# First feed-forward products with the high and low activations in one 512-column matmul

## The chip, the cores and the metric

One core of one Trainium2 chip runs the whole program. The metric is device time in microseconds (us), the median over several runs; lower is better. The profile beside it is one execution.

## The reference, cut to what matters

Two transformer-like blocks run one after the other on 256 rows of 2048 numbers, all in 32-bit floats. Both end with the same feed-forward, and only these two are touched:

```python
h2 = rms_norm(x, norm2_w) * (1.0 + scale2) + shift2      # 256 x 2048
f  = jnp.square(jax.nn.relu(h2 @ w_ff1)) @ w_ff2         # 2048 -> 8192 -> 2048
x  = x + gate2 * f
```

Shift, scale and gate come from `silu(c) @ w_ada`, one row times a 2048 x 12288 matrix for each block (the modulation). Before the feed-forwards stand the input projections, pooling and stick-breaking attention in the first block, dilated attention and a gated recurrence in the second, and their output projections.

## The kernel before, in words

**Precision.** TensorE multiplies numbers of the format fp32r, which keeps fewer bits than a 32-bit float. So each operand is split into a high part (rounded to fp32r) and a low part (the rest), and a product is taken as high x high + high x low + low x high: three matmuls that accumulate in PSUM. For the weights ScalarE (ACT in the profile) makes the high part `WH` by a copy (line 1000), and VectorE (DVE) makes the low part `WL` by a subtraction (line 1367). Lines 598, 1000, 1367 and 1375 are helpers, so they stand for nearly all matmuls, activations, tensor-tensor operations and scalar-tensor-tensor operations.

**The stream of weights.** All weights come in chunks of 256 x 512 numbers (512 KB), 848 of them, numbered j. SyncE issues their DMAs into a ring of raw buffers (`RAW`, `RAWX`, `RAWY`; six slots, four from chunk 434 to 591). The split halves have three slots each (a fourth in part of the second block). On every engine the program is one loop over j. ACT and DVE split chunk j+2 (`feed`, `look`) in their round j; ACT waits for the slot, that is, for PE to have finished chunk j-1. The modulation's weights travel in the same raw ring, as chunks that DVE multiplies by a column of `silu(c)` and adds up (`ACC<-RAW,CS,ACC`, line 1375); `weight_plan` spreads them over the weights: over the first 240 chunks of the first feed-forward in five groups with pauses, over the first 160 of the second in one.

**Blocks.** `block_table` lists the output blocks. A block of the second product (`ff2`, `fg2`) is 4 chunks and has rows of x as its output partitions: activations are stationary, weights move, 512 columns a matmul (`chunk`). A block of the first product (`ff1`, `fg1`) is 8 chunks and comes out transposed (`chunk_t`): weights are stationary (128 x 128), and the 256 rows of activations move, so each (k, i) step of a chunk is three matmuls of 256 columns (WH with high, WH with low, WL with high). Its output of 512 x 256 fills two PSUM banks, two i to a bank. `Blocks` gives each block a pair of banks, 0-1 and 2-3 in turn; banks 4 to 7 serve the side work (transposes, attention, recurrence). `prev` says which block had the pair before, and `bank_free` makes PE wait until that one was read.

**Order in a feed-forward.** Two blocks of the first product come first; then eight rounds: two blocks of the first product for the next round (none in the last round), then four blocks of the second product, which use what the first product made a round earlier. So 16 chunks of the one kind and 16 of the other take turns, and the last 32 chunks are all of the second kind.

**What happens to a finished block.** `ended(j)` hands the two halves (t = 0, 1) of a block to `evac` in the two rounds after its last chunk. For the first product ACT does Relu from PSUM into `rl`, Square into the high part `AH`, Square into `fs` (full precision), and DVE subtracts into the low part `AL`. For the second product DVE adds the PSUM bank to `acc` (in the first round of four ACT copies it there), and in the last rounds multiplies by the gate and adds into x.

**The norm before a feed-forward.** x is normalised, transposed on PE into banks 4 to 7 tile by tile (`turn_rows`), scaled and shifted by DVE into `hn` (`norm_tile`), copied as high part by ACT and subtracted as low part by DVE (`norm_low`); the first block's chunk c waits for the tile it uses.

Of the kernel before, what the change touches and what calls it, by code (L numbers as in the profile page):

```python
# [110 lines left out]
def f32(ap):  # L111
    return ap.bitcast(F32)
# [167 lines left out]
def reader(name, n):  # L280

    if name == "in1":
        return "dve" if n > 0 else "act"
    if name in ("oa", "ff1", "fg1"):
        return "act"
    if name in ("ff2", "fg2"):
        return "act" if n < 4 else "dve"
    if name == "in2":
        return "dve" if IN2_ORDER[n] // 2 in (3, 6) else "act"
    return "dve"  # L290


class Blocks:


    def __init__(self):
# [4 lines left out]
        self.sum_of, self.head = [], []  # L301
        counts, owner, pair, parts = {"act": 0, "dve": 0}, {}, 0, {}
        for q, (name, n, at, ticks) in enumerate(self.all):
            if (name, n) == ("in1", 0):
                b, pair = 0, 1
                self.first = q
            else:
                b = 2 * (pair % 2) + (2 if at < 64 else 0)
                pair += 1
            eng = reader(name, n)  # L310
            self.sum_of.append(parts.get(n) if name in ("part", "in1") else None)
            if name == "part":
                if n not in parts:
                    eng = "act"
# [6 lines left out]
            self.prev.append(owner.get(b))  # L321
            owner[b] = q
            self.by_end[at + ticks - 1] = q
            self.at[name, n] = q
# [21 lines left out]
def program(nc, I, C, out):  # L346
# [3 lines left out]
    with ExitStack() as ctx:  # L350
# [43 lines left out]
        def ff_memory(tag, stack):  # L394
            h = sb("BH" + tag, [128, KT, S], F32R, stack)
            l = sb("BL" + tag, [128, KT, S], F32R, stack)
            xn = sb("xn" + tag, [128, 2, D], F32, stack)
            hn = sb("hn" + tag, [128, 4, 256], F32, stack)
            acc = sb("acc" + tag, [128, 2, D], F32, stack)
            rl = sb("rl" + tag, [128, 2, 512], F32, stack)  # L400
            fs = sb("fs" + tag, [128, 2, 512], F32, stack)
            tmp = sb("tmp" + tag, [128, 2, 512], F32, stack)
            return {"h": h, "l": l, "xn": xn, "hn": hn, "acc": acc, "rl": rl, "fs": fs, "tmp": tmp}

# [98 lines left out]
        def vc(name, t=0):  # L503
# [24 lines left out]
            "cols", "sqrt", "rows0", "rows1", "turned", "mod", "hi", "lo")]  # L528
        s_fs, s_fl, s_fp = sem("f_square"), sem("f_lo"), sem("f_gated")
        s_ct, s_lb, s_lbe, s_gs, s_f, s_ln = (sem("ct_rounded"), sem("lb_step"), sem("lb_exp"), sem("gate_sigmoid"),  # L530
# [64 lines left out]
        def _(e):  # L595
# [7 lines left out]
            def bank_free(q, t):  # L603

                before = bl.prev[q]
                if before is not None:
                    eng, count = evac_of[before][t]
                    e.wait_ge(s_ev[eng], count)
# [16 lines left out]

            def chunk_t(j, q, c, hi, lo):
# [329 lines left out]
            for j in range(AUP, NW):  # L956
# [7 lines left out]
                if name in ("ff1", "fg1"):  # L964
                    mem, base = (M1, FF) if name == "ff1" else (M2, FG)
                    if n == 0:
                        e.wait_ge(s_nl, 8 * norms[base][0] + c + 1)
                    chunk_t(j, q, c, mem["h"], mem["l"])
                elif name in ("ff2", "fg2"):
# [27 lines left out]
        def _(e):  # L997
# [46 lines left out]
            def evac(q, t):  # L1044
# [3 lines left out]
                if name in ("in1", "part"):  # L1048
# [12 lines left out]
                    elif name == "in1" and n >= 12:  # L1061
                        g_b = SB[:, t, (n - 12) * 512:(n - 11) * 512]
                        e.wait_ge(s_ev["dve"], evac_of[q][t][1])
                        af(g_b, g_b, ACT.Sigmoid).then_inc(s_sgb, 1)
                elif name in ("ff1", "fg1"):
                    mem, base = (M1, 0) if name == "ff1" else (M2, 32)
                    r = n // 2
                    i = base + 2 * n + t
                    k = 8 * (r % 2) + 4 * (n % 2) + 2 * t
                    e.wait_ge(s_wdone, done_at)  # L1070
                    if n > 0:
                        e.wait_ge(s_fl, i - 1)
                    af(mem["rl"][:, t, :], ps, ACT.Relu).then_inc(s_ev["act"], 1)
                    e.wait_ge(s_ev["act"], evac_of[q][t][1])
                    af(AH[:, k:k + 2, :].rearrange("p a b -> p (a b)"), mem["rl"][:, t, :], ACT.Square)
                    af(mem["fs"][:, t, :], mem["rl"][:, t, :], ACT.Square).then_inc(s_fs, 1)
                elif name in ("ff2", "fg2") and n < 4:
# [20 lines left out]
                elif name == "oa":  # L1098
# [3 lines left out]
                    af(HG[:, 1 + n // 2, t, (n % 2) * 512:(n % 2) * 512 + 512], ps, ACT.Copy).then_inc(s_ev["act"], 1)  # L1102

            def squares(name, n, t):

# [17 lines left out]
            def norm_tile(at, i):  # L1123
                inst, _, _, hn, hi, _ = norms[at]
                e.wait_ge(s_nv, 16 * inst + 2 * i + 2)
                src = hn[:, 2 * i % 4:2 * i % 4 + 2, :].rearrange("p a s -> p (a s)")
                af(hi[:, 2 * i:2 * i + 2, :].rearrange("p a s -> p (a s)"), src, ACT.Copy).then_inc(s_nh, 1)

# [220 lines left out]
            for j in range(NW + 3):  # L1349
# [14 lines left out]
        def _(e):  # L1364
# [117 lines left out]
            def evac(q, t):  # L1482
# [35 lines left out]
                elif name in ("ff1", "fg1"):  # L1518
                    mem, base = (M1, 0) if name == "ff1" else (M2, 32)
                    k = 8 * (n // 2 % 2) + 4 * (n % 2) + 2 * t  # L1520
                    two = slice(k, k + 2)
                    e.wait_ge(s_fs, base + 2 * n + t + 1)
                    tt(AL[:, two, :].rearrange("p a b -> p (a b)"), mem["fs"][:, t, :],
                       f32(AH[:, two, :]).rearrange("p a b -> p (a b)"), ALU.subtract).then_inc(s_fl, 1)
                elif name in ("ff2", "fg2") and n >= 4:
# [49 lines left out]
                elif name == "ob":  # L1575
# [3 lines left out]
                    add_x("ob", n, t, ps, o, ev)  # L1579

            def gated_first(n, t):

# [19 lines left out]
            def norm_low(at, i):  # L1602
                inst, _, _, hn, hi, lo = norms[at]
                e.wait_ge(s_nh, 8 * inst + i + 1)
                two = slice(2 * i, 2 * i + 2)
                src = hn[:, 2 * i % 4:2 * i % 4 + 2, :].rearrange("p a s -> p (a s)")
                tt(lo[:, two, :].rearrange("p a s -> p (a s)"), src, f32(hi[:, two, :]).rearrange("p a s -> p (a s)"),
                   ALU.subtract).then_inc(s_nl, 1)

# [301 lines left out]
            for j in range(NW + 3):  # L1911
# [9 lines left out]
                else:  # L1921
# [143 lines left out]
```

## Time and profile before

| | us |
|---|---|
| median of 3 runs (2688.21 to 2689.26) | 2688.37 |
| profiled execution | 2683.85 |
| its span, first to last instruction | 2682.1 |
| PE busy | 2547.7 (95%) |
| DVE busy | 2000.3 (75%) |
| ACT busy | 1273.0 (47%) |

Engines: PE is TensorE's matmuls, PEld its weight loads, DVE is VectorE, ACT ScalarE, POOL GpSimd. Matmuls are pipelined and the printed lengths of neighbours overlap; the distance between two starts is the pace. An arrow reads output <- inputs, with the names of the program's tiles (`BH` and `BL` are the high and low activations here, `PS` is PSUM). The names of an instruction's tiles tell the stage: `PS<-BH,WH` is the first product, `PS<-WH,AH` the second product or another one with moving weights. In the chain of waits, "issue" is time for which the profile shows no reason.

### The profile page before, as it was taken

To read this page: it belongs to the slowest core of one execution; us is meant where nothing else is said; L and a number is where in the kernel's file an instruction comes from. 1 tells how busy PE (TensorE), PEld (TensorE's weight loads), DVE (VectorE), ACT (ScalarE), POOL (GpSimd) and SP (SyncE) were. 2 spreads that over 40 slices of the span, in tenths; PEclk is the share of its full clock that TensorE was granted. 3 is DMA by queue.
4 is the path that set the end of the run, shared out by engine and by line. 5 is a ranking of instruction groups with operands and counts; after the bars stand their busy time and mean duration, and the time that the engine had idled before them with its cause. 6 is when DMAs were issued, how large, how long until landed. Compare 5 with 4: busy or idle time off the path is not lost.

```text
span 2682.1 us, 36228 instructions
## 1 busy us (share of the span) xinstructions
PE 2547.7 (95%) x14307; PEld 2220.3 (83%) x14307; DVE 2000.3 (75%) x2232; ACT 1273.0 (47%) x1590; POOL 278.1 (10%) x323
## 2 busy tenths in 40 slices
PE   5999999998999999999989999888899999999998
PEld 4777777777999989998867788767799998999897
DVE  6788858998877888788888677876765566565556
ACT  4544395344454444444445544345445444444443
POOL 0000120202030201001030002451000000020000
PEclk9999999999999999999999999999999999999999
DMA  8998849997888989897965645666567777766664
GB/s 312 316 335 323 275 154 342 322 329 251 298 291 308 319 297 332 267 354 259 329 196 175 180 134 149 196 218 205 192 186 227 226 223 228 226 216 191 190 183 147
DMA packets 298218, 663.88 MB, mean 248 GB/s; under 512 B 20753, under 2 KB 20849, under 8 KB 297025
## 3 DMA queue, kind: packets, MB, share of 16 engines
q1 hardware_dynamic: 294976, 650.21, 72.9%
q0 software_dynamic: 2784, 10.05, 1.1%
q8 instruction: 113, 1.85, 0.3%
q10 hardware_dynamic: 288, 1.31, 0.1%
q14 instruction: 57, 0.46, 0.0%
HBM read 659.39 MB, written 2.10 MB: 247 GB/s over the span
## 4 chain that ended last, share of the span: by engine, by line
PE 75%; DVE 11%; issue 4%; DMA 4%; ACT 4%; POOL 1%; SPq 0%; DVEq 0%; ACTq 0%
PE PS L598 75%; DVE WL L1367 3%; DVE ACC L1375 3%; ACT WH L1000 2%; DMA RAW<-in_w_in 2%; DVE UQ L1367 1%; DMA RAWX<-in_w_ada 1%; DVE hn L1372 1%; PE PS L601 1%; DMA RAW<-in_w_o 0%; ACT L1000 0%; DMA RAWX<-in_w_a_up 0%; DVE acc L1367 0%; ACT UQ L1000 0%; DVE AL L1367 0%
## 5 line engine op out<-in xcount | busy, mean ns | idle before, releaser
L1367 DVE TENSOR_TENSOR WL<-RAW,WH 128x1024 fp32r<-128x1024 f32 x567 | 706.6, 1247 | 404.2 <-ACT WH L1000 403.7
L1000 ACT ACTIVATE WH<-RAW 128x1024 fp32r<-128x1024 f32 x567 | 600.8, 1060 | 831.4 <-PE PS L598 646.4
L598 PE MATMUL PS<-WH,AH 128*128 128x512 f32 x2052 | 815.5, 397 | 25.8 <-DVE WL L1367 12.4
L598 PE MATMUL PS<-WL,AH 128*128 128x512 f32 x2052 | 802.9, 391 | 0.0
L598 PE MATMUL PS<-WH,AL 128*128 128x512 f32 x2052 | 802.7, 391 | 0.0
L598 PE MATMUL PS<-BH,WH 128*128 128x256 f32 x2048 | 583.0, 285 | 5.1 <-DVE BL L1367 5.1
L598 PE MATMUL PS<-BH,WL 128*128 128x256 f32 x2048 | 581.4, 284 | 0.0
L598 PE MATMUL PS<-BL,WH 128*128 128x256 f32 x2048 | 581.4, 284 | 0.0
L598 PEld LDWEIGHTS PS<-WH,AH 128*128 128x128 f32 x2052 | 387.8, 189 | 116.8 <-DVE WL L1367 25.9
L598 PEld LDWEIGHTS PS<-WH,AL 128*128 128x128 f32 x2052 | 387.2, 189 | 82.3
L598 PEld LDWEIGHTS PS<-WL,AH 128*128 128x128 f32 x2052 | 387.7, 189 | 77.7 <-issue 1.0
L598 PEld LDWEIGHTS PS<-BH,WH 128*128 128x128 f32 x2048 | 394.9, 193 | 8.7 <-DVE BL L1367 8.2
L598 PEld LDWEIGHTS PS<-BL,WH 128*128 128x128 f32 x2048 | 394.9, 193 | 0.5
L598 PEld LDWEIGHTS PS<-BH,WL 128*128 128x128 f32 x2048 | 394.8, 193 | 0.0
L1375 DVE SCALAR_TENSOR_TENSOR ACC<-RAW,CS,ACC 128x1024 f32<-128x1024 f32 x265 | 338.6, 1279 | 2.5 <-DMA RAW<-in_w_ada 1.7
L1965 POOL PARTITION_ALL_REDUCE ACC<-ACC x72 | 156.0, 2250 | 1339.5 <-DVE ACC L1375 1339.5
L1000 ACT ACTIVATE WH<-RAWX 128x1024 fp32r<-128x1024 f32 x150 | 158.9, 1060 | 201.9 <-PE PS L598 131.3
L1367 DVE TENSOR_TENSOR WL<-RAWX,WH 128x1024 fp32r<-128x1024 f32 x150 | 187.7, 1252 | 63.0 <-ACT WH L1000 62.5
L1367 DVE TENSOR_TENSOR WL<-RAWY,WH 128x1024 fp32r<-128x1024 f32 x96 | 117.6, 1225 | 81.8 <-ACT WH L1000 81.8
L1000 ACT ACTIVATE WH<-RAWY 128x1024 fp32r<-128x1024 f32 x96 | 101.8, 1061 | 139.7 <-PE PS L598 136.4
L1375 DVE SCALAR_TENSOR_TENSOR ACC<-RAWX,CS,ACC 128x1024 f32<-128x1024 f32 x95 | 121.4, 1278 | 5.6 <-DMA RAWX<-in_w_ada 5.5
L598 PE MATMUL PS<-WX,AH 128*128 128x512 f32 x248 | 77.5, 394 | 2.1 <-DVE AL L1367 2.1
(241 smaller groups left out, 2033.3 us busy)
## 6 DMA issues: line engine op xcount, KB each, us to landing
RAW<-in_w_ff SPq DMA_DIRECT2D x335, 512.0 KB, 4.6
RAW<-in_w_ada SPq DMA_DIRECT2D x284, 512.0 KB, 5.1
RAW<-in_w_in SPq DMA_DIRECT2D x192, 512.0 KB, 4.5
RAWX<-in_w_ada SPq DMA_DIRECT2D x100, 512.0 KB, 5.5
RAWY<-in_w_ff SPq DMA_DIRECT2D x96, 512.0 KB, 4.5
RAWX<-in_w_ff SPq DMA_DIRECT2D x81, 512.0 KB, 5.0
RAWX<-in_w_in SPq DMA_DIRECT2D x48, 512.0 KB, 5.3
RAW<-in_w_out SPq DMA_DIRECT2D x32, 512.0 KB, 4.3
```

Source lines behind the costliest of these rows:

```text
L598: return e.matmul(o, l, r, start=start, stop=stop, skip_group_check=True)
L601: return e.transpose(o, i, ident)
L1000: return e.activation(o, i, f, **kw)
L1367: return e.tensor_tensor(o, a, b, op)
L1372: return e.tensor_scalar(o, a, s1, s2, op0, op1)
L1375: return e.scalar_tensor_tensor(out=o, in0=a, scalar=s, in1=b, op0=op0, op1=op1)
L1965: e.partition_all_reduce(part, part, 128, bass.bass_isa.ReduceOp.add).then_inc(s_red, 1)
```

## The change

The high and the low activations of the feed-forward lie side by side in one tile `HL`, so that for each k the 256 high and the 256 low columns are one run of 512. `chunk_t` sends both through WH in one matmul of 512 columns, whose output is a whole bank, and the high ones through WL in a second matmul of 256 columns, which adds to the first half of that bank. The low activations' share thus stands in the second half, apart. A block takes one bank for each i, four in all: 0 to 3 or 4 to 7 in turn; the blocks of the second product rotate over all eight banks. After a block ACT copies the second halves of two banks to `rl`, DVE adds the first halves to them in place, ACT takes Relu in place and both Squares a round later (`ff_square`), and DVE subtracts into `AL` two rounds later (`ff_low`). The second block of each feed-forward waits until the norm has read banks 4 to 7. The norm's copies and subtractions write into `HL` in two runs of 256.

```diff
@@ reader @@
-    if name in ("oa", "ff1", "fg1"):
+    if name == "oa":
         return "act"
@@ Blocks.__init__ @@
+            elif name in ("ff1", "fg1"):
+                b = 4 * (n % 2)
+            elif name in ("ff2", "fg2"):
+                b = 2 * (n % 4)
...
+            if name in ("ff1", "fg1"):
+                self.prev.append([owner[b // 2 + t][1] for t in range(2)])
+                for t in range(2):
+                    owner[b // 2 + t] = [self.ev[q][t]] * 2
+            else:
+                self.prev.append(owner[b // 2])
+                owner[b // 2] = self.ev[q]
@@ ff_memory @@
-            h = sb("BH" + tag, [128, KT, S], F32R, stack)
-            l = sb("BL" + tag, [128, KT, S], F32R, stack)
+            hl = sb("HL" + tag, [128, KT, 2, S], F32R, stack)
@@ tensor: chunk_t @@
-                        o = PS[:, b + i // 2, (i % 2) * 256:(i % 2) * 256 + 256]
-                        mm(o, h, hi[:, k, :], k == 0 and i % 2 == 0, False)
-                        mm(o, h, lo[:, k, :], False, False)
-                        m = mm(o, l, hi[:, k, :], False, k == KT - 1)
+                        mm(PS[:, b + i, :], h, both[:, k, :, :].rearrange("p a s -> p (a s)"), k == 0, False)
+                        m = mm(PS[:, b + i, 0:256], l, both[:, k, 0, :], False, k == KT - 1)
@@ tensor: main loop @@
+                    elif n == 1 and c == 0:
+                        e.wait_ge(s_nv, 16 * norms[base][0] + 16)
@@ scalar: evac @@
-                    if n > 0:
-                        e.wait_ge(s_fl, i - 1)
-                    af(mem["rl"][:, t, :], ps, ACT.Relu).then_inc(s_ev["act"], 1)
-                    e.wait_ge(s_ev["act"], evac_of[q][t][1])
-                    af(AH[:, k:k + 2, :].rearrange("p a b -> p (a b)"), mem["rl"][:, t, :], ACT.Square)
-                    af(mem["fs"][:, t, :], mem["rl"][:, t, :], ACT.Square).then_inc(s_fs, 1)
+                    two = PS[:, bl.bank[q] + 2 * t:bl.bank[q] + 2 * t + 2, 256:512]
+                    if n > 0:
+                        e.wait_ge(s_fs, base + 2 * n + t - 1)
+                    af(mem["rl"][:, t, :].rearrange("p (a s) -> p a s", s=256), two, ACT.Copy).then_inc(s_fc, 1)
+            def ff_square(q, t):
...
+                e.wait_ge(s_ev["dve"], evac_of[q][t][1])
+                af(mem["rl"][:, t, :], mem["rl"][:, t, :], ACT.Relu).then_inc(s_fr, 1)
+                e.wait_ge(s_fr, i + 1)
+                af(AH[:, k:k + 2, :].rearrange("p a b -> p (a b)"), mem["rl"][:, t, :], ACT.Square)
+                if n > 0:
+                    e.wait_ge(s_fl, i - 1)
+                af(mem["fs"][:, t, :], mem["rl"][:, t, :], ACT.Square).then_inc(s_fs, 1)
@@ scalar: loop, after feed(j + look(j)) and before evac @@
+                for q, t in bl.ended(j - 1):
+                    if bl.all[q][0] in ("ff1", "fg1"):
+                        ff_square(q, t)
@@ vector: evac @@
-                    e.wait_ge(s_fs, base + 2 * n + t + 1)
-                    tt(AL[:, two, :].rearrange("p a b -> p (a b)"), mem["fs"][:, t, :],
-                       f32(AH[:, two, :]).rearrange("p a b -> p (a b)"), ALU.subtract).then_inc(s_fl, 1)
+                    two = PS[:, bl.bank[q] + 2 * t:bl.bank[q] + 2 * t + 2, 0:256]
+                    low = mem["rl"][:, t, :].rearrange("p (a s) -> p a s", s=256)
+                    e.wait_ge(s_fc, base + 2 * n + t + 1)
+                    tt(low, two, low, ALU.add).then_inc(s_ev["dve"], 1)
@@ vector: loop, after feed and before evac; ff_low holds the subtraction removed above @@
+                    for q, t in bl.ended(j - 2):
+                        if bl.all[q][0] in ("ff1", "fg1"):
+                            ff_low(q, t)
```

## Rows read from the trace of the kernel before

**Rows 1.** The page's busy time (us, share of the span, instructions) of each engine.
```profile
PE 2547.7 (95%) x14307; PEld 2220.3 (83%) x14307; DVE 2000.3 (75%) x2232; ACT 1273.0 (47%) x1590; POOL 278.1 (10%) x323
```

**Rows 2.** The chain that ended last: start, us, what; its two longest pieces.
```profile
693.07 612.87 PE PS L598 x4080
...
1972.95 699.94 PE PS L598 x4464
```

**Rows 3.** The same chain from 640 to 720: one period of the head.
```profile
679.90 0.99 DVE hn L1372 x2
...
681.49 1.08 DVE ACC L1375
...
683.74 0.99 DVE hn L1372 x2
```

**Rows 4.** Stretches: length, then busy us (count) by engine, PE clock, DMA share, GB/s.
```profile
669.00:672.00 3.00, 3.00 (x14) 3.00 (x15) 2.99 (x5) 0.63 (x1) 0.00 (x0) 0.50 0.00 0
...
768.04:811.59 43.55, 43.55 (x195) 36.06 (x193) 27.56 (x25) 23.15 (x28) 20.79 (x8) 1.00 0.75 250
811.59:857.66 46.07, 46.07 (x385) 46.07 (x384) 35.38 (x32) 21.23 (x24) 0.00 (x0) 1.00 0.92 315
...
1126.52:1170.07 43.55, 43.55 (x195) 36.05 (x193) 40.27 (x39) 20.15 (x22) 0.00 (x0) 1.00 0.99 355
...
1259.69:1305.76 46.07, 46.07 (x385) 46.07 (x384) 37.51 (x34) 20.27 (x22) 0.00 (x0) 1.00 0.97 346
1305.76:1353.90 48.14, 44.62 (x195) 35.69 (x193) 46.75 (x49) 20.25 (x22) 5.42 (x3) 1.00 0.80 272
...
1972.95:2672.90 699.95, 699.92 (x4464) 639.68 (x4464) 413.02 (x391) 319.19 (x353) 20.08 (x14) 1.00 0.67 208
```

**Rows 5.** PE in order of time: start us, length us, operation; where widths change.
```profile
669.34 0.41 PE L598 MATMUL PS<-BL,WH 128*128 128x256 f32 x1
669.55 0.41 PE L598 MATMUL PS<-BH,WL 128*128 128x256 f32 x1
...
767.92 0.28 PE L598 MATMUL PS<-BH,WL 128*128 128x256 f32 x1
768.04 0.40 PE L598 MATMUL PS<-WH,AH 128*128 128x512 f32 x1
...
811.36 0.39 PE L598 MATMUL PS<-WH,AL 128*128 128x512 f32 x1
811.59 0.28 PE L598 MATMUL PS<-BH,WH 128*128 128x256 f32 x1
...
1601.95 1.05 PE L598 MATMUL PS<-QP,KP 128*128 128x128 f32 x8
```

**Rows 6.** DVE in order of time in a busy stretch, and PE's matmul after it.
```profile
1151.63 0.68 DVE L1367 TENSOR_TENSOR acc<-PS,acc 128x512 f32<-128x512 f32 x1
1152.23 1.27 DVE L1375 SCALAR_TENSOR_TENSOR ACC<-RAWX,CS,ACC 128x1024 f32<-128x1024 f32 x1
1153.42 1.22 DVE L1367 TENSOR_TENSOR WL<-RAW,WH 128x1024 fp32r<-128x1024 f32 x1
1154.56 0.68 DVE L1367 TENSOR_TENSOR acc<-PS,acc 128x512 f32<-128x512 f32 x1
...
1156.38 1.23 DVE L1367 TENSOR_TENSOR WL<-RAW,WH 128x1024 fp32r<-128x1024 f32 x1
...
1159.19 0.39 PE L598 MATMUL PS<-WH,AH 128*128 128x512 f32 x1
```

**Rows 7.** ACT in order of time, the end of a first-product block.
```profile
1130.79 0.58 ACT L1000 ACTIVATE rl<-PS 128x512 f32<-128x512 f32 x1
1131.40 0.63 ACT L1000 ACTIVATE AH<-rl 128x512 fp32r<-128x512 f32 x1
1131.93 0.61 ACT L1000 ACTIVATE fs<-rl 128x512 f32<-128x512 f32 x1
1132.45 1.04 ACT L1000 ACTIVATE WH<-RAWX 128x1024 fp32r<-128x1024 f32 x1
```

More of the change, by code:

```diff
@@ L301, in __init__ @@
         self.sum_of, self.head = [], []
-        counts, owner, pair, parts = {"act": 0, "dve": 0}, {}, 0, {}
+        counts, owner, pair, parts = {"act": 0, "dve": 0}, [[None, None] for _ in range(4)], 0, {}
         for q, (name, n, at, ticks) in enumerate(self.all):
@@ L320, in __init__ @@
             counts[eng] += 2
-            self.prev.append(owner.get(b))
-            owner[b] = q
+            if name in ("ff1", "fg1"):
[5 more added lines that the diff above has]
+                owner[b // 2] = self.ev[q]
             self.by_end[at + ticks - 1] = q
@@ L402, in ff_memory @@
             tmp = sb("tmp" + tag, [128, 2, 512], F32, stack)
-            return {"h": h, "l": l, "xn": xn, "hn": hn, "acc": acc, "rl": rl, "fs": fs, "tmp": tmp}
+            return {"hl": hl, "h": hl[:, :, 0, :], "l": hl[:, :, 1, :], "xn": xn, "hn": hn, "acc": acc, "rl": rl, "fs": fs, "tmp": tmp}
         phase = ExitStack()
@@ L528, in program @@
             "cols", "sqrt", "rows0", "rows1", "turned", "mod", "hi", "lo")]
-        s_fs, s_fl, s_fp = sem("f_square"), sem("f_lo"), sem("f_gated")
+        s_fc, s_fr, s_fs, s_fl, s_fp = sem("f_low_part"), sem("f_relu"), sem("f_square"), sem("f_lo"), sem("f_gated")
         s_ct, s_lb, s_lbe, s_gs, s_f, s_ln = (sem("ct_rounded"), sem("lb_step"), sem("lb_exp"), sem("gate_sigmoid"),
@@ L603, in bank_free @@
             def bank_free(q, t):
-                before = bl.prev[q]
+                before = bl.prev[q][t]
                 if before is not None:
-                    eng, count = evac_of[before][t]
+                    eng, count = before
                     e.wait_ge(s_ev[eng], count)
@@ L624, in chunk, with chunk_t @@
                 m.then_inc(s_wdone, 1)
-            def chunk_t(j, q, c, hi, lo):
+            def chunk_t(j, q, c, both):
                 e.wait_ge(s_lo, j + 1)
@@ L967, in _ @@
                         e.wait_ge(s_nl, 8 * norms[base][0] + c + 1)
-                    chunk_t(j, q, c, mem["h"], mem["l"])
+                    elif n == 1 and c == 0:
+                        e.wait_ge(s_nv, 16 * norms[base][0] + 16)
+                    chunk_t(j, q, c, mem["hl"])
                 elif name in ("ff2", "fg2"):
@@ L1102, in evac @@
                     af(HG[:, 1 + n // 2, t, (n % 2) * 512:(n % 2) * 512 + 512], ps, ACT.Copy).then_inc(s_ev["act"], 1)
+            def ff_square(q, t):
+                name, n = bl.all[q][:2]
+                mem, base = (M1, 0) if name == "ff1" else (M2, 32)
+                i = base + 2 * n + t
+                k = 8 * (n // 2 % 2) + 4 * (n % 2) + 2 * t
+                e.wait_ge(s_ev["dve"], evac_of[q][t][1])
[5 more added lines that the diff above has]
+                af(mem["fs"][:, t, :], mem["rl"][:, t, :], ACT.Square).then_inc(s_fs, 1)
             def squares(name, n, t):
@@ L1125, in norm_tile @@
                 e.wait_ge(s_nv, 16 * inst + 2 * i + 2)
-                src = hn[:, 2 * i % 4:2 * i % 4 + 2, :].rearrange("p a s -> p (a s)")
-                af(hi[:, 2 * i:2 * i + 2, :].rearrange("p a s -> p (a s)"), src, ACT.Copy).then_inc(s_nh, 1)
+                af(hi[:, 2 * i:2 * i + 2, :], hn[:, 2 * i % 4:2 * i % 4 + 2, :], ACT.Copy).then_inc(s_nh, 1)
             def norm_begin(at):
@@ L1579, in evac, with ff_low @@
                     add_x("ob", n, t, ps, o, ev)
+            def ff_low(q, t):
+                name, n = bl.all[q][:2]
+                mem, base = (M1, 0) if name == "ff1" else (M2, 32)
+                k = 8 * (n // 2 % 2) + 4 * (n % 2) + 2 * t
+                two = slice(k, k + 2)
+                e.wait_ge(s_fs, base + 2 * n + t + 1)
+                tt(AL[:, two, :].rearrange("p a b -> p (a b)"), mem["fs"][:, t, :],
+                   f32(AH[:, two, :]).rearrange("p a b -> p (a b)"), ALU.subtract).then_inc(s_fl, 1)
             def gated_first(n, t):
@@ L1605, in norm_low @@
                 two = slice(2 * i, 2 * i + 2)
-                src = hn[:, 2 * i % 4:2 * i % 4 + 2, :].rearrange("p a s -> p (a s)")
-                tt(lo[:, two, :].rearrange("p a s -> p (a s)"), src, f32(hi[:, two, :]).rearrange("p a s -> p (a s)"),
-                   ALU.subtract).then_inc(s_nl, 1)
+                tt(lo[:, two, :], hn[:, 2 * i % 4:2 * i % 4 + 2, :], f32(hi[:, two, :]), ALU.subtract).then_inc(s_nl, 1)
             def norm_begin(at):
```

5 lines of the change are left out of this document (removed).

## The prediction

> **What bounds the kernel now.** I read the busy table first: PE is busy 95% of the span, DVE 75%, ACT 47% [rows 1]. A share that high for PE is only a hint, so the chain of waits comes next. Its two longest pieces are PE alone: 612.87 us from 693.07, and 699.94 us from 1972.95, half of the span together [rows 2]. These are the two feed-forwards. In them nothing but the number and the spacing of the matmuls sets the time. Two stretches at their edges are different. At the head of each feed-forward, before 693 and before 1973, the chain runs through DVE: a normalised tile is scaled, its low part made, one modulation product added, in 3.8 us per chunk [rows 3]. (A chunk is one 256 x 512 piece of weights, a block is 8 chunks of the first product or 4 of the second.) At the tail of the first feed-forward, 1305.76 to 1353.90, DVE is busy 46.75 of 48.14 us and PE waits for it [rows 4].
>
> **The spacing of matmuls.** The lengths printed for matmuls overlap, so I take start-to-start spacings. Sixteen chunks of the first product are 384 matmuls of 256 columns in 46.07 us, 120.0 ns each; sixteen of the second are 192 of 512 columns in 43.55 us, 226.8 ns each [rows 4]. At the granted clock of 1.00 (2.4 GHz) the columns alone would take 106.7 and 213.3 ns. Both widths pay the same 13.3 to 13.5 ns on top, and both load their weights anew each time. So this is a surcharge per matmul, not per column. Where widths change, a 256 is followed after 0.12 us by a 512, and a 512 after 0.23 us by a 256 [rows 5], as in the uniform streams. Eight matmuls of 128 columns with own weights take 1.05 us [rows 5]: under 0.13 each, and some 0.11 when the overhang of the last is taken off, although their columns would take 0.053. That is the nearest thing to a floor from weight loading; it is under 0.12, so the loads still hide behind the 256-column stream, which the change keeps as the shortest one.
>
> **What the change takes from PE.** Before, each (k, i) step is three matmuls of 256 columns, 360.0 ns. After, it is one of 512 and one of 256, 226.8 + 120.0 = 346.8 ns: 13.2 ns less. A chunk has 8 such steps, 0.105 us of 2.88. Each feed-forward has 128 chunks of the first product. The first six run in the DVE-bound head, and the first of these at a granted clock of 0.50 [rows 4], where starts are 0.21 us apart, 256 columns at 1.2 GHz and no surcharge to save [rows 5]; I count nothing for them. That leaves 2 x 122 = 244 chunks, 1952 steps, 25.7 us. The bounds: with the boundary rows as printed, 0.23 + 0.12 = 0.35 us, a step saves 0.010 us, 19.5 us in all. More than 13.2 ns is excluded, because every width in the trace pays the surcharge. A gain below nothing is excluded for PE by itself, since no spacing gets longer than in the streams shown.
>
> The Trainium skill, "TensorE: Matmul & The Clock Gate", section "Back-to-back issue gap", gives a warm gap of N/2.4 + 2.5 ns. By that a step would save 2.5 ns and the whole 4.9 us. The trace does not agree: it has 13.3 ns over the stream in both widths [rows 4].
>
> **What it adds to ACT and DVE.** A block's end was, for each of two halves: ACT Relu from PSUM, Square into AH, Square into fs, then DVE's subtraction into AL. Now ACT first copies the low-part half-banks, DVE adds the other halves, ACT does Relu and both Squares one chunk later, and DVE's subtraction comes two chunks later. So each half adds one PSUM read on ACT (0.61 us from one start to the next, as the Relu has) and one PSUM addition on DVE (0.60 us, as acc<-PS,acc has) [rows 6, 7]. Per feed-forward that is 16 blocks x 2 x 0.60 = 19 us of DVE. In the second feed-forward DVE is busy 413 of 700 us [rows 4], and the weights' low parts are ready well ahead; cost nothing. In the first one there are modulation products besides, and the question is whether the low part WL of a chunk is still ready when PE wants it. The tightest place I found: WL ends at 1157.61 and PE begins that chunk at 1159.19, a lead of 1.6 us [rows 6].
>
> By hand, from the spacings of rows 6 and 7 (WL 1.14, product 1.19, addition or subtraction 0.60, weight copy 0.97 to 1.06, Relu 0.61, Squares 0.53 and 0.52), with a chunk every 2.72 us and a product in every one: let chunk A begin at 0. ACT copies weights until 1.3 and the low parts until 1.9; DVE adds until 3.2. In B, ACT has weights until 4.0, Relu and Squares until 5.6, the second copy until 6.2; DVE, ready before, waits 0.7 us for it and adds until 6.9. In C, ACT begins the weights at 6.2 instead of 5.7; DVE has the product until 8.0 and WL at 9.2, wanted at 10.9: lead 1.7. Then 1.5 in D, 1.3 in E, 1.0 in F, and 0.8 at the lowest, with the subtractions and the second product's additions in between. Products come in fewer than all chunks, so the lead recovers. Taken alone this gives no stall. What can turn it into one is late weights: in this very stretch the DMA engines are busy 0.99 at 355 GB/s. Products and first-product chunks together draw 346 GB/s at 2.88 us a chunk [rows 4]; at 2.775 that becomes 359, at what the queue was ever seen to hold (355 / 0.99 = 359). I allow 1.2 us of new PE waits there. The bounds are 0 (the rings of six raw and three split buffers take it up) and 8 us (0.5 us at each of 16 blocks).
>
> At the tail DVE is the chain, so what is added there is paid. The last first-product block ends at 1305.8, and its two additions fall into it: 2 x 0.60, with 0.1 for the later handover: 1.3 us, between 0 and 3.
>
> The banks: blocks of the first product now hold four banks, 0 to 3 or 4 to 7, and those of the second rotate over all eight. The owner before ended at least 8 chunks (22 us) earlier in each case, where it could be 4 before; in the norm stage banks 4 to 7 belong to the transposes until the second block, which waits for all 16 tiles. The last tile is done before the head ends, two chunks before that block begins. Nothing for either.
>
> **The sum.** 2683.85 (the profiled execution) - 25.7 + 1.3 + 1.2 = 2660.65 us. The median of the runs is 2688.37, 4.52 above the profiled execution, and I add that: 2665.2 us.
>
> **The rivals.**
> - *Half the gain is taken by weight delivery in the first feed-forward.* For it: the 355 GB/s above, and PE already gets along with a lead of 1.6 us. Against it: a group of products lasts about 37 chunks and then pauses, and the excess of demand over supply is under 1%. If it holds, the first feed-forward keeps its pace: 2688.4 - 12.9 + 1.3 = 2676.8.
> - *The surcharge is owed for each 256 columns, or is far smaller in a mixed stream.* Then the step is as long as before and only the tail moves: 2688.4 + 1.3 = 2689.7; with the page's 2.5 ns it would be 2684.8. Against it: 226.8 ns for 512 columns, where two surcharges would make 240.
> - *Slower: the new round trip ACT, DVE, ACT, DVE blocks ACT's weight copies.* ACT works in order, its Relu waits for DVE's addition, which stands behind a low part and a product, and the weight copy of the next chunk is queued behind. For it: DVE is busy 92 to 97% in the densest stretches [rows 4]. Against it: the leads above, and the second feed-forward has no products after its first 160 chunks. It decides from 0.8 us of PE waiting at every one of the 32 blocks (25.7 / 32). With 1.2 us at each, 2688.4 - 25.7 + 1.3 + 38.4 = 2702.4.
>
> **How the numbers follow.** The forecast has 0.84, weight delivery 0.08, the surcharge 0.03, slower 0.05. With everything at its best the forecast's case gives 2688.4 - 25.7 = 2662.7, with everything at its worst 2688.4 - 19.5 + 8 + 3 = 2679.9; its own range is 2661 to 2672, since the 4.5 us between profile and median may shift by a microsecond or two and the worst ends hardly meet. The range for 8 in 10 takes in a little of the second case: 2660.5 to 2673. A change of 0.2%, 5.4 us, is about what can be told from none here. Faster by more has the first two cases, 0.92; within it the third, 0.03; slower 0.05.
>
> **What would show it.** In the changed profile: sixteen chunks of the first product in 44.4 us instead of 46.07; a pair spacing of 0.23 and 0.12; PE busy without a gap from about 693, ending the long piece some 12.8 us sooner, and the second one shortened by the same. ACT's copies and DVE's additions 64 times each, near 0.58 and 0.68 us. The tail from the last first-product block to the norm longer than now by about 1.3 us. I am wrong on the size if sixteen chunks take more than 45 us, and on the mechanism if PE shows waits for WL after each first-product block.

## The result

The changed kernel takes 2669.45 us in the median of 4 runs (2666.06 to 2675.75), against 2688.29 us for the kernel before in the same comparison. The ratio is 0.9936, with a 95% interval of 0.9918 to 0.9954: 12 to 22 us less, where 23.2 were forecast (2665.2 us, range 2660.5 to 2673). The direction and the range held. The size of the main term did not: by the forecast's own sign (sixteen chunks over 45 us) it was wrong on the size.

The profile after: first the busy time of each engine (answers to [rows 1]), then the two longest pieces of the chain ([rows 2]).

```profile
PE 2536.4 (95%) x12259; PEld 2111.6 (79%) x12259; DVE 2035.6 (76%) x2296; ACT 1300.1 (49%) x1654; POOL 287.3 (11%) x323
```

```profile
696.22 611.98 PE PS L607 x3128
...
1972.57 692.22 PE PS L607 x3488
```

The 2048 matmuls taken away are there (14307 to 12259), and so are 35 us more of DVE. The second piece, which ends with the last chunk in both kernels, is 7.7 us shorter. The first can't be compared by its length, since it ends at another chunk. By chunks (198 to 415 in both) it went from 612.69 to 606.30 us. First the row of before, then those of after: the same chunks, then sixteen second-product chunks, sixteen first-product ones, two stretches of the second feed-forward, and the first half of the tail ([rows 4]).

```profile
693.07:1305.76 612.69, 612.69 (x4080) 567.75 (x4081) 496.85 (x462) 283.95 (x317) 71.75 (x32) 1.00 0.88 307
```

```profile
696.22:1302.52 606.30, 606.30 (x3105) 515.42 (x3106) 512.02 (x492) 296.61 (x347) 76.32 (x32) 1.00 0.88 309
...
769.81:813.34 43.53, 43.53 (x195) 36.05 (x193) 30.92 (x27) 23.97 (x30) 20.19 (x8) 1.00 0.74 250
813.34:858.55 45.21, 45.21 (x258) 39.22 (x256) 36.46 (x34) 22.14 (x26) 0.00 (x0) 1.00 0.92 315
2000.41:2044.79 44.38, 44.38 (x259) 38.82 (x258) 28.09 (x27) 25.17 (x32) 0.00 (x0) 1.00 0.73 226
2088.33:2133.54 45.21, 45.21 (x258) 39.23 (x256) 25.86 (x24) 22.03 (x26) 0.00 (x0) 1.00 0.71 224
1302.52:1352.93 50.41, 45.00 (x194) 35.57 (x193) 48.14 (x51) 21.07 (x24) 5.41 (x3) 1.00 0.78 273
```

PE is busy without a gap in all stretches but the tail. Yet sixteen chunks of the first product take 45.21 us, not 44.4: only 0.86 us less than before. One stretch, from 2000.41, takes 44.38, exactly as forecast. The same instructions thus ran at two paces, at the same granted clock of 1.00. PE in order of time shows them (start, length, operation). First the slow one; three steps of a 512 and a 256 take 1.06 us (719.63 to 720.69), 353 ns each, and the 512s keep the next matmul away for 0.24, 0.24 and 0.23 us:

```profile
719.63 0.40 PE L607 MATMUL PS<-HL,WH 128*128 128x512 f32 x1
719.87 0.28 PE L607 MATMUL PS<-HL,WL 128*128 128x256 f32 x1
719.99 0.40 PE L607 MATMUL PS<-HL,WH 128*128 128x512 f32 x1
720.23 0.28 PE L607 MATMUL PS<-HL,WL 128*128 128x256 f32 x1
720.34 0.40 PE L607 MATMUL PS<-HL,WH 128*128 128x512 f32 x1
720.57 0.28 PE L607 MATMUL PS<-HL,WL 128*128 128x256 f32 x1
720.69 0.40 PE L607 MATMUL PS<-HL,WH 128*128 128x512 f32 x1
```

In the fast one two steps take 0.69 us (2009.77 to 2010.46), 346 ns each:

```profile
2009.77 0.40 PE L607 MATMUL PS<-HL,WH 128*128 128x512 f32 x1
2010.00 0.28 PE L607 MATMUL PS<-HL,WL 128*128 128x256 f32 x1
2010.12 0.39 PE L607 MATMUL PS<-HL,WH 128*128 128x512 f32 x1
2010.35 0.27 PE L607 MATMUL PS<-HL,WL 128*128 128x256 f32 x1
2010.46 0.40 PE L607 MATMUL PS<-HL,WH 128*128 128x512 f32 x1
```

In nanoseconds the spacings repeat as 241, 120, 236, 113, 233, 117 in the slow rhythm (1060 for three steps) and as 231, 112, 233, 117 in the fast one (693 for two). Over sixteen chunks that is 353.2 and 346.7 ns a step. In this profile 26 of the 244 chunks ran in the fast one.

### The profile page after: what moved, and what is told of

It is laid out like the page before. It is cut to its first block, busy times and chain, and to the rows that moved or that the text cites. A ratio compares the mean times of both kernels' runs of the same rounds, so it can differ in the third digit from the quotient of the medians.

```text
span 2674.0 us, 32260 instructions
## 1 busy us (share of the span) xinstructions
PE 2536.4 (95%) x12259; PEld 2111.6 (79%) x12259; DVE 2035.6 (76%) x2296; ACT 1300.1 (49%) x1654; POOL 287.3 (11%) x323
## 4 chain that ended last, share of the span: by engine, by line
PE 77%; DVE 9%; ACT 4%; issue 4%; DMA 4%; POOL 1%; SPq 0%; DVEq 0%; ACTq 0%
PE PS L607 76%; DVE WL L1388 2%; DVE ACC L1396 2%; ACT WH L1010 2%; DMA RAW<-in_w_in 2%; DVE UQ L1388 1%; DMA RAWX<-in_w_a_up 1%; PE PS L610 1%; DMA RAWX<-in_w_ada 1%; DVE hn L1393 1%; POOL NT L1974 1%; ACT L1010 0%; POOL NT L1979 0%; DVE acc L1388 0%; ACT UQ L1010 0%
## 5 line engine op out<-in xcount | busy, mean ns | idle before, releaser
L607 PE MATMUL PS<-HL,WH 128*128 128x512 f32 x2048 | 728.7, 400 | 5.6 <-DVE HL L1388 5.6
L607 PE MATMUL PS<-HL,WL 128*128 128x256 f32 x2048 | 576.2, 281 | 0.0
L607 PEld LDWEIGHTS PS<-HL,WH 128*128 128x128 f32 x2048 | 386.9, 189 | 104.1 <-DVE HL L1388 9.0
L607 PEld LDWEIGHTS PS<-HL,WL 128*128 128x128 f32 x2048 | 388.8, 190 | 0.5
L1995 POOL PARTITION_ALL_REDUCE ACC<-ACC x72 | 162.2, 2336 | 1325.9 <-DVE ACC L1396 1325.9
L1974 POOL TENSOR_SCALAR NT<-SM 128x4 f32<-128x4 f32 (+2 forms) x14 | 16.0, 1141 | 470.3 <-DVE SM L1399 411.7
L1388 DVE TENSOR_TENSOR acc<-PS,acc 128x512 f32<-128x512 f32 x96 | 65.6, 683 | 0.0
```

The source lines that it names most:

```text
L607: return e.matmul(o, l, r, start=start, stop=stop, skip_group_check=True)
L1388: return e.tensor_tensor(o, a, b, op)
L1974: e.tensor_scalar(o, a, s1, s2, ALU.mult, ALU.add).then_inc(s_rs, 1)
L1995: e.partition_all_reduce(part, part, 128, bass.bass_isa.ReduceOp.add).then_inc(s_red, 1)
```

## The experiments

Their timings belong to three comparisons with the kernel before, whose medians lay at 2686.4 us (the first four experiments), 2687.7 (the next four) and 2687.0 (the last four). Single runs have no interval, so only their profiles are used. In what follows "sixteen chunks" is the length of a first-product stretch in the profile.

**The same kernel again.** No edit.

> The changed kernel once more. In its first profile a pair of matmuls (512 and 256 columns) took 346.3 ns in the first 26 chunks of the second feed-forward and 353.2 ns in the other 218, where 346.8 was forecast. Theory A (the alternation of widths has two steady rhythms, and which one a stretch gets is chance): the profile again has stretches at 2.77 and at 2.83 us a chunk, but elsewhere; the times scatter over some 10 us as before (2666 to 2676), since all fast against all slow is 244 x 0.055 = 13 us. Theory B (the rhythm is fixed by the place in the program): the same 26 chunks are fast again, the rest slow, and the times scatter by 2 us only.

Measured: 2669.62 us (4 runs, 2668.95 to 2674.14), ratio 0.9942 (0.9927 to 0.9957). The first 26 chunks of the first feed-forward, slow before, were fast now (44.38 us, first row), the first 26 of the second fast again, and every later stretch slow in both profiles:

```profile
721.70:766.08 44.38, 44.38 (x259) 38.81 (x258) 40.49 (x39) 25.17 (x32) 0.00 (x0) 1.00 0.97 345
809.68:854.88 45.20, 45.20 (x257) 39.20 (x256) 36.44 (x34) 22.15 (x26) 0.00 (x0) 1.00 0.91 314
```

So neither theory holds whole: the stretches entered from the head of a feed-forward have either rhythm, and the twelve entered from the second product's 512s always had the slow one. What the rhythm can explain between two runs is 2 x 26 chunks, 2.7 us at most. The other scatter is older than the change: the kernel before ranged from 2680.22 to 2691.34 us over 13 runs in this comparison, and the first 192 chunks, which the change doesn't touch, took 624.7 to 630.7 us in all the profiles, counted from the first matmul with weights.

**The block end alone.** The merged matmul is split into two again.

```diff
-                        mm(PS[:, b + i, :], h, both[:, k, :, :]..., k == 0, False)
+                        mm(PS[:, b + i, 0:256], h, both[:, k, 0, :], k == 0, False)
+                        mm(PS[:, b + i, 256:512], h, both[:, k, 1, :], False, False)
                         m = mm(PS[:, b + i, 0:256], l, both[:, k, 0, :], False, k == KT - 1)
```

> The changed kernel with its merged matmul undone: WH with the high columns and WH with the low columns are again two matmuls of 256 columns, into the two halves of the bank. Banks, copies, additions and their delays stay as changed. This is the cost of the new block end by itself. Theory A and B alike: chunks at 2.880 us in all of both feed-forwards, no scatter, and against the kernel before only the tail of the first feed-forward grows: 1.3 us forecast, 1.9 seen in the first profile; 2689 to 2691 us. Rival C (the new block end also slows matmuls beside it, through the shared banks): chunks longer than 2.880 us near the block ends, over 2692 us.

Measured: 2689.48 us (10 runs) against 2686.38 (13 runs), ratio 1.0011 (1.0001 to 1.0021), 0.3 to 5.6 us slower. All stretches are those of the kernel before, and the tail is longer:

```profile
817.10:863.17 46.07, 46.07 (x385) 46.06 (x384) 36.20 (x33) 22.14 (x26) 0.00 (x0) 1.00 0.91 309
1311.27:1361.33 50.06, 44.96 (x194) 35.58 (x193) 48.03 (x51) 21.08 (x24) 5.40 (x3) 1.00 0.79 271
```

The new block end slows no matmul beside it, so rival C falls. Nor do the new banks: with them a stream of 256s still takes 46.07 us. The whole gain comes from the merged matmul. The first half of the tail is 1.7 to 1.9 us longer than in the two profiles of before; the rest of this profile's 9 us over the first of them lies mostly in the first 192 chunks (5.0) and the heads (1.3), which scatter.

**Four 512s, then four 256s.** The second matmul moves into a loop of its own over i.

> As the changed kernel, but for each k the four matmuls of 512 columns come first and the four of 256 after them, so widths change twice in eight matmuls instead of eight times. Theory A (the alternation has the slow rhythm): chunks at 8 x (226.8 + 120.0) = 2.774 us in nearly all stretches, so 218 x 0.055 = 12 us less than the changed kernel's profile, 2662 to 2666 us, and little scatter. Rival D (the surcharge grows for another reason, as for a moving operand read twice in a row or for the state of the chip): still 2.83 us in most stretches, 2668 to 2676 us.

Measured: 2666.7 us (4 runs), ratio 0.9931 (0.9915 to 0.9948). Sixteen chunks take 44.88 us in every stretch but the first of each feed-forward (44.91), half-way between. Both theories had it wrong: grouping helps, but a run of four 512s behind 256s is spaced 233, 236, 228, 233 or 235, 234, 236, 224 ns, so it does not settle at 226.7.

**The 256 first in each pair.**

> As the changed kernel, but in each pair the 256 columns with WL come first and the 512 with WH second. Theory A: the same alternation, so both rhythms are possible again, 2.77 or 2.83 us a chunk, 2664 to 2677 us with scatter. Rival E (what costs is that a matmul of 256 follows one of 512 into the same bank): the 256 now precedes the 512 of its bank and follows one of another bank, and all chunks take 2.774 us, 2662 to 2666 us.

Measured: 2674.41 us (4 runs, 2667.96 to 2675.55), ratio 0.9951 (0.9937 to 0.9966). Sixteen chunks take 45.22 us in all fourteen stretches. Rival E falls: the slow pace stays where the 256 no longer follows the 512 of its own bank.

The row of the fours, then that of the 256 first:

```profile
808.69:853.57 44.88, 44.88 (x257) 39.24 (x256) 35.91 (x33) 22.15 (x26) 0.00 (x0) 1.00 0.90 314
```

```profile
815.25:860.47 45.22, 45.22 (x257) 39.21 (x256) 36.12 (x33) 22.15 (x26) 0.00 (x0) 1.00 0.92 313
```

**The kernel before again.** No edit.

> The kernel before once more, for a second profile of it. The changed kernel and its first variants showed the first chunk of both feed-forwards at 5.2 to 5.7 us against 4.97 and 4.87 in the one profile of before, and 193 to 194 us for the first 64 chunks of the program against 191.7. Theory A (these parts have nothing to do with the change and scatter): they differ again, the first chunk over 5.2 us. Theory B (the change costs half a microsecond at each head): 4.9 us again. Both: every first-product chunk at 2.880 us.

Measured: 2686.78 us (one run). Theory A: the first chunk of the second feed-forward took 5.82 us up to the next one's start this time, as long as the longest with any variant of the change (5.83), and that of the first 4.83. How long PE stays at a granted clock of 0.50 after the gap there is scatter:

```profile
812.55:858.62 46.07, 46.07 (x386) 46.07 (x385) 35.62 (x32) 21.24 (x24) 0.00 (x0) 1.00 0.90 315
1306.72:1355.06 48.34, 44.69 (x194) 35.65 (x193) 46.83 (x49) 20.26 (x22) 5.41 (x3) 1.00 0.79 269
1951.28:1957.10 5.82, 5.82 (x29) 5.82 (x29) 2.73 (x4) 0.88 (x3) 0.00 (x0) 0.52 0.31 90
```

In two profiles of variants (the mirrored pairs, and the last one of eights) one of the two first chunks had a granted clock of 1.00 throughout and took 3.3 us. The one of the mirrored pairs:

```profile
670.50:673.76 3.26, 3.26 (x21) 2.88 (x21) 3.21 (x5) 0.74 (x3) 0.00 (x0) 1.00 0.02 5
```

**Mirrored pairs.** For odd i the 256 comes first, then the 512.

> The changed kernel with every second pair turned round: 512, 256, 256, 512, 512, 256, 256, 512. Widths change four times in eight matmuls instead of eight. Where four 512s stood together (and two changes in eight) a chunk took 2.805 us, at eight changes 2.83 or 2.77. If each change of width costs the same, this lies between, 2.81 to 2.82 us a chunk, 45.1 us for sixteen. If it is a beat of the sequence as a whole, it can be anything from 2.774 up, and the spacings repeat in a pattern of their own.

Measured: 2665.13 us (one run). Sixteen chunks take 44.58 us, less than with fours. Four changes of width cost less than two did, so it is no fixed price per change but depends on the whole sequence; the spacings repeat every four steps, a pattern of their own, as the second expectation had it.

```profile
809.28:853.86 44.58, 44.58 (x257) 38.94 (x256) 36.43 (x34) 22.12 (x26) 0.00 (x0) 1.00 0.92 316
```

**Eight 512s, then eight 256s.** One loop over both k and all i for the 512s, one for the 256s.

> All eight 512s of a chunk first, then its eight 256s: two changes of width in sixteen matmuls. If the extra time sits in the first few matmuls after a change (in the variant with fours a 512 after the 256s is 233 to 236 ns from the next, in the second product it settles at 226.7 after about five), a chunk takes 2.79 us and the median is 2664 to 2667 us. If it stays for as long as 256s are in the mix, 2.80 to 2.83 us as with fours or alone, 2667 to 2671 us.

Measured: 2663.08 us (4 runs), ratio 0.9914 (0.9898 to 0.9929). Sixteen chunks take 44.66 us, 2.79 us each, as the first expectation said: after 256s the 512s stand 232, 236, 228, 233 and 231 ns apart and then 226 to 227, with the 256s at 120 again after two.

```profile
809.39:854.05 44.66, 44.66 (x257) 39.35 (x256) 36.44 (x34) 22.12 (x26) 0.00 (x0) 1.00 0.91 318
```

**Entry from 256s.** The first chunk of the first of two blocks is three matmuls of 256 columns.

> The changed kernel, but the first chunk of each pair of first-product blocks is three matmuls of 256 columns again, so the alternation is entered from a stream of 256s, not from the 512s of the second product. Every stretch entered from 512s had the slow rhythm (2.83 us a chunk) in three profiles, those entered from the head of a feed-forward had either. Theory A (the entry sets the rhythm, and it then stays): the stretches from the third round on change to 2.77 us, 44.5 us for sixteen chunks with the thin one counted, about 2660 to 2664 us. Rival (the slow rhythm is where every stretch ends up once ACT, DVE or the queue have their steady state): 45.3 us for sixteen, 2670 us.

Measured: 2673.13 us (4 runs), ratio 0.9947 (0.9931 to 0.9964). Sixteen chunks take 45.27 us in all stretches, so theory A falls: entry from 256s gives the slow rhythm too. The rival's forecast came true, but its cause, the steady state of the other engines, is not shown by that.

```profile
809.54:854.81 45.27, 45.27 (x266) 39.66 (x264) 36.43 (x34) 22.16 (x26) 0.00 (x0) 1.00 0.92 313
```

What picks the fast rhythm stays open. It was seen only where PE starts after a wait, behind the head of a feed-forward. With the two runs below that keep the alternation, five profiles have ten such stretches, and six were fast: two of five in the first feed-forward and four of five in the second.

**Denser products before the tail.**

```diff
-    ... [ada1[5], ada2[0], ada2[1], ada2[3], ada2[4]], 0, 240)
+    ... [ada1[5], ada2[0], ada2[1], ada2[3], ada2[4]], 0, 228)
```

> The changed kernel with the five groups of modulation products spread over the first 228 chunks of the first feed-forward instead of 240, so that they end 12 chunks before the tail's middle and come 5% denser before. Chunks 416 to 448 took 105.1 to 106.6 us with the new block end and 103.9 and 105.8 in two profiles of before. Theory A (the tail is bound by DVE's products and low parts, and the change is paid there only for that): 98 to 102 us in the tail. Theory B (the tail is bound by the raw ring, which has four slots from chunk 434): over 104 us. For the rival of the forecast, that weight delivery is at its edge in the stretches with products: the second-product stretches then take over 44 us for sixteen chunks instead of 43.58; if it has room, 43.6.

Measured: 2669.08 us (one run). In the profile chunks 416 to 432 took 47.74 us instead of 50.41, and 432 to 448 stayed (55.63 after 55.46), 103.4 together: between the two theories. DVE's products bind the first half of the tail, but not the second, which took as long as before. Most second-product stretches kept 43.58, two rose: the one from 766.89 by 1.0 us, another by 0.2.

```profile
766.89:811.45 44.56, 44.14 (x194) 35.88 (x193) 32.57 (x28) 25.03 (x31) 16.97 (x8) 1.00 0.74 245
...
1300.79:1348.53 47.74, 45.12 (x194) 35.50 (x193) 45.67 (x51) 21.26 (x25) 18.27 (x8) 1.00 0.51 177
```

**A doubled addition.**

```diff
-                    tt(low, two, low, ALU.add).then_inc(s_ev["dve"], 1)
+                    tt(low, two, low, ALU.add).then_inc(s_dd, 1)
+                    e.wait_ge(s_dd, base + 2 * n + t + 1)
+                    tt(low, low, low, ALU.max).then_inc(s_ev["dve"], 1)
```

> The changed kernel with a second DVE operation of the same size (a maximum of rl with itself, 128x512) behind every addition of a first-product block, so the round trip ACT, DVE, ACT, DVE is 0.7 us longer in each half. If the hand calculation of the forecast is right (the lead of WL falls to 0.8 us at the lowest with a product in every chunk), stretches outside the tail still show no PE waits or less than 0.3 us each, 45.2 and 43.6 us for sixteen chunks, and only the tail grows, by 2 x 0.7 = 1.4 us to some 107 us. If the round trip was near to blocking (the slower rival), the second-product stretches of the first feed-forward take 44 to 45 us, those of the second still 43.6.

Measured: 2673.61 us (one run). Three stretches of the first feed-forward grew: by 1.1 (from 767.07), by 0.5 (from 1123.33, the one where the DMA engines are busiest), and the first-product one from 721.50 by 1.2 us against the fast rhythm in which it began. All others stayed, those of the second feed-forward too. So the lead is used up here and there, but not at every block. The first half of the tail took 50.42 us, where 1.4 more than without the doubling were expected; the variants without it took 49.7 to 51.0, so DVE's share in the tail's growth isn't settled by this run.

```profile
767.07:811.74 44.67, 43.85 (x194) 35.97 (x193) 34.06 (x30) 23.97 (x30) 19.06 (x8) 1.00 0.77 253
...
1123.33:1167.41 44.08, 43.90 (x194) 35.97 (x193) 41.62 (x42) 21.30 (x24) 0.00 (x0) 1.00 0.97 351
1301.42:1351.84 50.42, 44.96 (x194) 35.57 (x193) 49.39 (x53) 21.21 (x24) 5.40 (x3) 1.00 0.77 277
```

The stretch from 721.50 shows more than the total tells: how a wait comes about, and what it does to the rhythm. Weights had come 2.7 us late at a block's end. ACT's Relu, two Squares and the copy of low parts followed the weight copy, so DVE waited 0.96 us for that copy (row at 751.75). Its addition, the added maximum and a product, 2.5 us, then went ahead of the next low part `WL` (754.28), and PE stood for 0.62 us (755.56; in brackets the wait). The last two rows are three chunks before it and two after (columns as above):

```profile
751.75 0.69 DVE L1389 TENSOR_TENSOR rl<-PS,rl 128x512 f32<-128x512 f32 x1 [0.96 <-ACT rl L1011]
754.28 1.22 DVE L1389 TENSOR_TENSOR WL<-RAW,WH 128x1024 fp32r<-128x1024 f32 x1
755.56 0.50 PE L608 MATMUL PS<-HL,WH 128*128 128x512 f32 x1 [0.62 <-DVE WL L1389]
743.68:752.00 8.32, 8.32 (x50) 7.28 (x49) 6.42 (x8) 5.04 (x8) 0.00 (x0) 1.00 1.01 384
761.42:767.07 5.65, 5.65 (x34) 4.90 (x33) 5.65 (x5) 2.12 (x2) 0.00 (x0) 1.00 0.98 327
```

Before the wait a chunk took 2.77 us, at the end of the stretch 2.82 to 2.83. The chunk right behind the wait was still fast; the slow rhythm began behind a second, shorter gap of 0.05 us one chunk later. So the alternation went in fast and came out slow, inside one stretch. The first of these rows also has the DMA engines at 384 GB/s, more than the 359 that the forecast took for the most they were seen to hold.

**Sixteens and eights.** Eights with the two groups turned round in odd chunks:

```diff
+                for low in ((False, True) if c % 2 == 0 else (True, False)):
+                    for kk in range(2):
+                        for i in range(4):
+                            ...  # the 256 with WL if low, else the 512 with WH
```

> Eights with the order turned round in every second chunk: eight 512s, sixteen 256s, sixteen 512s and so on, one change to 512 in two chunks. In the variant with eights the five 512s after 256s cost 5, 10, 2, 6 and 4 ns over 226.7, and two 256s 7 and 1 under 120, 18 ns a chunk net. If that is paid once per change, a chunk takes 2.783 us, sixteen take 44.5, and the median is 2 us under eights. If the rhythm has other long patterns, anything up to 44.9.

> The variant with eight 512s and eight 256s per chunk again, beside the sixteens and with more rounds. Both theories: 44.67 us for sixteen chunks in every stretch of the profile as in its first, and a median of 2662 to 2667 us.

Measured: sixteens 2662.47 us (4 runs, 2660.46 to 2664.99), ratio 0.9909 (0.9894 to 0.9924); eights 2663.0 us (4 runs), ratio 0.991 (0.9893 to 0.9927). Sixteen chunks take 44.53 and 44.67 us, as expected of both (the first such stretch of the eights took 44.94); the timings can't tell the two apart.

```profile
808.47:853.00 44.53, 44.53 (x257) 39.36 (x256) 36.15 (x34) 22.09 (x26) 0.00 (x0) 1.00 0.92 318
```

In the eights the second-product stretch from 767.98 lost 0.8 us. The rows are ACT, DVE and PE in order of time, in brackets the wait:

```profile
773.23 1.06 ACT L1013 ACTIVATE WH<-RAWX 128x1024 fp32r<-128x1024 f32 x1 [2.42 <-DMA RAWX<-in_w_ff]
774.20 0.62 ACT L1013 ACTIVATE rl<-rl 128x512 f32<-128x512 f32 x1
775.90 0.58 ACT L1013 ACTIVATE rl<-PS 128x512 f32<-128x512 f32 x1
776.38 1.05 ACT L1013 ACTIVATE WH<-RAW 128x1024 fp32r<-128x1024 f32 x1
776.51 0.69 DVE L1391 TENSOR_TENSOR rl<-PS,rl 128x512 f32<-128x512 f32 x1 [0.96 <-ACT rl L1013]
777.12 1.27 DVE L1399 SCALAR_TENSOR_TENSOR ACC<-RAWX,CS,ACC 128x1024 f32<-128x1024 f32 x1
778.32 1.22 DVE L1391 TENSOR_TENSOR WL<-RAW,WH 128x1024 fp32r<-128x1024 f32 x1
779.59 0.50 PE L607 MATMUL PS<-WH,AH 128*128 128x512 f32 x1 [0.54 <-DVE WL L1391]
```

Weights come 2.4 us late just at a block's end. Relu, the two Squares and the copy of the next low parts follow on ACT, and DVE waits 0.96 us for that copy. Its addition and a product then go ahead of the next `WL`, for which PE waits. It is not the wait that the slower rival described: ACT's Relu did not wait for DVE here, and the weight copy that this `WL` uses had ended at 777.43, 0.9 us before `WL` began.

## Why the prediction was right, and where it was not

**PE's spacing.** The step "one of 512 and one of 256, 226.8 + 120.0 = 346.8 ns" is the term that was mis-sized. In the changed kernel's profile it was 346.7 ns in 26 chunks and 353.2 ns in 218. The long stretches became 6.4 us (612.69 to 606.30) and 7.7 us (699.94 to 692.22) shorter, 14.1 where 25.7 were forecast; 218 chunks of 8 steps at 6.5 ns more are 11.3 of the 11.6 us that are missing. The spacings of two uniform streams were added, on the strength of single boundary rows [rows 5]: a 256 to a 512, 0.12 us, and a 512 to a 256, 0.23. Those are right, but they show only the first spacing behind a uniform stream, and the later ones grow (after the 512s the first step still took 227 and 113, then 233 and 117, then 241 and 120). "No spacing gets longer than in the streams shown" was the false sentence, and the trace of before already spoke against it. Behind the 256s the first five 512s, from 768.04 [rows 5] to this row, took 1.16 us, 232 ns each (234, 236, 227, 233, 231) where the stream settles at 226.7:

```profile
769.20 0.39 PE L598 MATMUL PS<-WH,AL 128*128 128x512 f32 x1
```

With sixteens a step takes 44.53 / 128 = 347.9 ns, and the long stretches are 23.8 us shorter than before: nearly all of the 25.7. So the surcharge per matmul was read rightly. What was not seen is that a quick change of widths has a price of its own, up to 6.4 ns a step. It is the widths and not the changing operands: in the second product `WH` and `WL`, `AH` and `AL` alternate too, all at 512 columns, and the spacing stays at 226.7.

**The rule of the page.** The Trainium skill's 2.5 ns in "TensorE: Matmul & The Clock Gate", "Back-to-back issue gap", would have given 4.9 us. The same section says that this is the gap of an isolated matmul and that in a stream of weight loads and matmuls both set the spacing, which the prediction left out. The measured 12 to 22 us exclude 4.9 for this kernel, and so do the 14.1 us in the long stretches.

**The block end.** 64 copies and 64 additions, at 0.58 and 0.69 us, as forecast. Undone to this part alone the kernel loses 0.3 to 5.6 us; 1.3 + 1.2 were forecast. The tail (chunks 416 to 448) took 105.1 to 106.6 us in the changed kernel's two profiles and eight variants with undoubled additions and the products as before, 103.9 and 105.8 in two profiles of before: about 1 us, with a scatter as large. Its first half alone grew clearly, from 48.1 and 48.3 to 49.7 to 51.0.

**New waits for weights.** 1.2 us were allowed, between 0 and 8. The changed kernel's two profiles and seven variants with undoubled additions show none outside the tail; the eights in their second profile lost 1.1 us (0.8 in one stretch, 0.3 in the one before), the denser products 1.2. The place is the one named, late weights meeting a block's end, and the doubled addition shows how near it is.

**The heads.** Nothing was counted. In the profile of after they are 1.1 us longer, but the second profile of before was 0.8 us longer than the first there, and first chunks ranged from 3.3 to 5.8 us over all profiles: scatter.

**The rivals.** Half the gain lost to weight delivery: the size nearly came, 14 instead of 25.7, but by another cause, and in both feed-forwards alike. That a step hardly gets shorter in a mixed stream: this is what it was, in part; it had 0.03, and was put as all or nothing. Its reason was the wrong way round: two matmuls of the slow rhythm pay 353.2 - 320.0 = 33.2 ns over their columns, more than the 26.7 of uniform streams, not less. Slower by the round trip: not here; with a doubled addition PE waited, but the chain to it ran from late weights through DVE, not through a blocked weight copy.

**The range.** That the median fell inside it is partly luck. With the measured terms in place of the forecast ones, 14.1 for PE and 1.9 for the tail, the forecast's sum gives 2688.4 - 14.1 + 1.9 = 2676.2 us, outside the range of 2660.5 to 2673. The repeated profile, with both first stretches fast, has 15.4 instead of 14.1, which gives 2674.9 at the same tail. The measured gain of 12 to 22 us takes in 12 to 15; what the median has above that is within the scatter of parts that the change does not touch.

The median fell by 18.8 us and the profiled spans by 8.1 (2682.1 to 2674.0). The profiled execution, 2675.75, was the slowest of the four. In it there was 14.1 less in the two long stretches, 1.9 more in the tail, and 4.1 more in heads, the first 192 chunks and the rest, which scatter by that much between profiles of one kernel.

## What to carry to other kernels

Where PE is the bound and every matmul loads its own weights, fewer and wider matmuls pay, and the distance between starts of matmuls, not their lengths, tells how much. Take that distance from a stream that has the new kernel's order; adding up two uniform streams can overstate the gain by nearly a factor of two, as here (25.7 for 14.1). Where two widths have to be mixed, try several orders: sixteen chunks took 45.21 us alternating and 44.53 with sixteens, and the ratio to the kernel before went from 0.9942 (0.9927 to 0.9957) to 0.9909 (0.9894 to 0.9924). Longer runs of one width mostly helped, but the number of changes does not tell the cost: mirrored pairs (44.58) were quicker than eights (44.66). A stream that seems steady can change its pace behind a short wait.

## What the runs showed of the hardware

With own weights each time, at a granted clock of 1.00, matmuls of 256 and 512 columns start 120.0 and 226.7 ns apart in uniform streams, 13.3 ns over the time of their columns. In mixed orders a step of one 512 and one 256 takes 353.2 or, less often, 346.7 ns when they alternate, 348.3 mirrored, 350.6 in fours, 348.9 in eights, 347.9 in sixteens. The alternating stream has at least two steady rhythms and kept the one it had for as long as PE did not wait; in the one case where it waited within a stretch (0.62 us, and 0.05 a chunk later) it changed over from the fast to the slow one. Behind 256s a stream of 512s is spaced 234, 236, 227, 233 and 231 ns before it settles. At a granted clock of 0.50, 256 columns start 0.21 us apart, without the surcharge. What in the engine makes the rhythm was not found.
